# One 512-column operand for x and ctx in the key and value projection of a fused two-block transformer kernel

## The reference, cut to what matters

```python
def mixer_inputs(h, w_in_l, conv_l, ...):
    p = h @ w_in_l                       # (256, 1024) @ (1024, 2576)
    u = p[..., :512]
    qkv = silu(dwconv1d(p[..., 512:2048], conv_l))
    z = p[..., 2048:2560]
    ab = p[..., 2560:2576]               # 16 columns: the small projection
    ...
def first_block(x, c, ctx, c_ctx, w_ada, ...):
    mod_l = silu(c) @ w_ada + b_ada      # modulation vectors, 6 x 1024
    mod_c = silu(c_ctx) @ w_ada + b_ada
    hl = rmsnorm(x, g) * (1 + scale_l) + shift_l
    hc = rmsnorm(ctx, g) * (1 + scale_c) + shift_c
    ul, zl, ql, kl, vl, bl, gl = mixer_inputs(hl, ...)
    uc, zc, qc, kc, vc, bc, gc = mixer_inputs(hc, ...)   # of ctx only k, v and the gates are used
    ...
```

## Time and profile before

| what | value |
|---|---|
| time of the runs | 1788.62 us median of 3 (1787.31 to 1790.93) |
| span of the profiled execution, first to last instruction | 1786.7 us |
| the profiled execution's own time | not listed beside the span; the median stands 1.9 us above the span |
| mean granted TensorE clock | 0.988 of full speed |
| TensorE matmul busy | 1704.3 us, 95% of the span |
| VectorE busy | 1097.3 us, 61% |
| ScalarE busy | 813.0 us, 46% |

### The profile page before, as it was taken

One profiled execution on the slowest core, in us unless ns is written; L12 is line 12 of the kernel. 1 busy time (PEld: TensorE's weight loads), 2 busy tenths in 40 slices (PEclk: granted clock), 3 DMA queues, 4 the chain that ended last, 5 costly groups with the idle time before them and its releaser, 6 DMA issues.

```text
span 1786.7 us, 34649 instructions
## 1 busy us (share of the span) xinstructions
PE 1704.3 (95%) x15394; PEld 1606.0 (90%) x15394; DVE 1097.3 (61%) x1367; ACT 813.0 (46%) x1051; POOL 34.2 (2%) x68
## 2 busy tenths in 40 slices
PE   5998899999999899999999999999999999999997
PEld 4896788799988899999999899979999999979997
DVE  3476664679853565468775755555447778666463
ACT  3245414433333535447654444435454575445352
POOL 0000000000000000000000000000000000000000
PEclk8998999999999999999999999999999999999999
DMA  9676433654568444445555355525444445535552
GB/s 397 254 279 235 183 147 128 235 191 167 201 224 328 173 164 162 139 149 178 177 189 182 117 191 196 189 98 186 142 142 165 165 166 189 189 110 185 200 189 71
DMA packets 45210, 329.32 MB, mean 184 GB/s; under 512 B 5008, under 2 KB 5008, under 8 KB 5392
## 3 DMA queue, kind: packets, MB, share of 16 engines
q1 hardware_dynamic: 35712, 258.63, 41.8%
q0 software_dynamic: 9216, 67.11, 9.8%
q10 hardware_dynamic: 144, 1.51, 0.2%
HBM read 326.18 MB, written 1.05 MB: 183 GB/s over the span
## 4 chain that ended last, share of the span: by engine, by line
PE 81%; DVE 9%; ACT 6%; DMA 2%; issue 1%; POOL 0%; SPq 0%; ACTq 0%; DVEq 0%; POOLq 0%
PE ps L342 20%; PE ps L344 20%; PE ps L343 20%; PE ps L395 4%; DVE w_lo L1607 3%; PE ps L467 3%; ACT w_hi L1071 3%; PE ps L446 3%; DMA ada_raw<-ada 2%; PE ps L630 1%; PE ps L641 1%; DVE rstd L1654 1%; DVE x L1692 1%; PE ps L973 1%; DVE rsq L2334 1%
## 5 line engine op out<-in xcount | busy, mean ns | idle before, releaser
L1607 DVE TENSOR_TENSOR w_lo<-raw,w_hi 128x2048 fp32r<-128x2048 f32 x207 | 474.5, 2292 | 489.4 <-ACT w_hi L1071 489.0
L342 PE MATMUL ps<-act_hi,w_hi 128*128 128x256 f32 x2672 | 756.6, 283 | 15.0 <-DVE act_lo L1676 4.6
L343 PE MATMUL ps<-act_lo,w_hi 128*128 128x256 f32 x2672 | 744.9, 279 | 0.0
L344 PE MATMUL ps<-act_hi,w_lo 128*128 128x256 f32 x2672 | 744.8, 279 | 0.0
L1071 ACT ACTIVATE w_hi<-raw 128x2048 fp32r<-128x2048 f32 (+1 forms) x229 | 421.7, 1842 | 551.5 <-PE ps L344 549.0
L342 PEld LDWEIGHTS ps<-act_hi,w_hi 128*128 128x128 f32 x2672 | 504.1, 189 | 25.3 <-issue 16.3
L343 PEld LDWEIGHTS ps<-act_lo,w_hi 128*128 128x128 f32 x2672 | 505.4, 189 | 1.1 <-issue 0.2
L344 PEld LDWEIGHTS ps<-act_hi,w_lo 128*128 128x128 f32 x2672 | 503.6, 188 | 0.0
L342 PE MATMUL ps<-mlp_hi,w_hi 128*128 128x256 f32 x512 | 143.0, 279 | 0.2
L343 PE MATMUL ps<-mlp_lo,w_hi 128*128 128x256 f32 x512 | 141.5, 276 | 0.0
L344 PE MATMUL ps<-mlp_hi,w_lo 128*128 128x256 f32 x512 | 141.5, 276 | 0.0
(11 more groups left out here) (407 smaller groups left out, 2053.3 us busy)
## 6 DMA issues: line engine op xcount, KB each, us to landing
raw<-stream SPq DMA_DIRECT2D x233, 1024.0 KB, 4.9
ada_raw<-ada POOLq DMA_DIRECT2D x64, 1024.0 KB, 7.0
ada_f<-ada SPq DMA_DIRECT2D x4, 1024.0 KB, 14.9
ada_a<-ada SPq DMA_DIRECT2D x3, 1024.0 KB, 20.6
consts_stage<-consts_a SPq DMA_DIRECT2D x1, 1728.0 KB, 32.7
consts_stage<-consts_b ACTq DMA_DIRECT2D x1, 1472.0 KB, 10.6
x<-xT SPq DMA_DIRECT2D x1, 1024.0 KB, 7.9
xc<-ctxT SPq DMA_DIRECT2D x1, 1024.0 KB, 9.9
```

Source lines behind the costliest of these rows:

```text
L342: mm(out, ah, bh, start=first, stop=False, skip_group_check=shared)
L343: mm(out, ah, bl, start=False, stop=False, skip_group_check=shared)
L344: return mm(out, al, bh, start=False, stop=last, skip_group_check=shared)
L1607: tt(w_lo[:, s2, :], raw[:, s4, :], w_hi[:, s2, :].bitcast(f32), ALU.subtract).then_inc(S("lo_ready"), 1)
```

## The change

The four activation buffers become one tensor of the same bytes, `act_parts`, indexed by part (high, low) and by token set (ctx, x). For KV0 to KV3 a new function issues one pass of 512 columns (256 of ctx, 256 of x, two runs 8 KB apart in a partition) for each weight tile where two passes of 256 stood. An output tile `b` now fills a whole bank, and ScalarE's copy reads the banks with the two token sets inside a bank. The work that stood between the two halves of KV0 goes behind KV0, and that inside KV1 goes ahead of KV1. The wait for the last ctx tile goes ahead of KV0.

```diff
-        act_hi = [at(f"act_hi{i}", [P, KT, T], F[i], f32r) for i in range(2)]
-        act_lo = [at(f"act_lo{i}", [P, KT, T], F[2 + i], f32r) for i in range(2)]
+        act_parts = at("act_parts", [P, 2, 2, KT, T], F[0], f32r)
+        act_hi, act_lo = ([act_parts[:, part, i, :, :] for i in range(2)] for part in range(2))
...
+            def both_chunk(wp, bank):
+
+                for b in range(2):
+                    for k in range(KT):
+                        o = (b * KT + k) * P
+                        last = mm3(ps[:, bank + b, :], w_hi[:, wp, o:o + P], w_lo[:, wp, o:o + P],
+                                   act_parts[:, 0, :, k, :], act_parts[:, 1, :, k, :], k == 0, k == KT - 1)
+                return last
...
             for c in range(4):
                 n = N_KV + c
                 begin(n, n)
-                bank = KV_BANK[c]
-                feat_chunk(n % 2, bank + 1, 1)
+                if c == 0:
+                    pe.wait_ge(S("mod_lo"), 16)
+                if c == 1:
+                    pe.wait_ge(S("ab_rows"), 1)
+                    small_tr(ab_rows, 4, 16).then_inc(S("ab_mm"), 1)
+                both_chunk(n % 2, KV_BANK[c]).then_inc(S("chunk_done"), 1)
                 if c == 0:
                     pe.wait_ge(S("sw_wide"), 1)
-                    pe.wait_ge(S("mod_lo"), 16)
                     small_mm(xc, 0)
                     small_mm(norm_h1, T).then_inc(S("ab_rows_mm"), 1)
                     ada_mm(1)
-                if c == 1:
-                    pe.wait_ge(S("ab_rows"), 1)
-                    small_tr(ab_rows, 4, 16).then_inc(S("ab_mm"), 1)
-                feat_chunk(n % 2, bank, 0).then_inc(S("chunk_done"), 1)
                 ada_mm(2 + c)
...
                 act_(pre_kv[:, 2 * c:2 * c + 2, :, 1:T + 1],
-                     ps[:, bank:bank + 2, :].rearrange("p s (b t) -> p b s t", b=2), ACT.Copy).then_inc(S("evicted"), 1)
+                     ps[:, bank:bank + 2, :].rearrange("p b (s t) -> p b s t", s=2), ACT.Copy).then_inc(S("evicted"), 1)
```

## The result

The changed kernel takes 1793.58 us (median of 7 runs, 1790.29 to 1798.61), the kernel before 1785.31 (7 runs, 1780.05 to 1790.93): ratio 1.0056, 95% interval 1.0039 to 1.0073. That is slower by 10 us (0.0056 x 1785.3), with 7 to 13 in the interval. The prediction was +5.6. Its absolute time, 1794.2, lies close to the measured one by luck: its base, 1788.62 from three runs, was 3.3 above what seven runs give. Its sign and the wait that it named were right, its size was about half, and one of its steps was wrong.

A forecast was written before the change was run, and what follows sets the result against it. The prediction took TensorE, with 81% of the chain, to bound the kernel. It summed +6.5 (KV1 begins late), +1.5 (clock) and -2.4 (KV1 to KV3) to +5.6: 1788.6 + 5.6 = 1794.2 us, range 1790.0 to 1798.5.

The forecast's parts named there:

- the wait that it named: Ahead of KV1, `ada_mm(2)` right behind `ada_mm(1)` waits for its refill; TensorE idle from 73.9 to 79.0.
- Step 1: Ahead of KV0: the first wide pass needs all ctx tiles, so KV0 starts at about 59.75, +2.4 us.
- Step 2: KV0 to KV3: 192 wide passes at 0.215 us each save 1.0 us in KV0 and 2.4 in KV1 to KV3.
- width gains nothing: Rival for KV0 to KV3: a wide pass takes 0.236 us, 3.4 us of gain are lost, 1797.6; chance 0.10.
- Step 3: Behind KV0: `small_mm` 1.75 us, `ada_mm(1)` 1.87 without its 1.17 wait; refills issued at 73.4 and 74.2.
- Step 4: `ada_mm(2)` waits for refills landing at 79.0 and 81.5; KV1's work begins at 82.5, +6.5 us including earlier delays and savings.
- Step 5: Half clock behind TensorE's idle time at `ada_mm(2)` costs 1.5 us, bounds 0 and 3; nothing for the gap ahead of KV0.
- Edits at no cost: ScalarE's copy, `small_tr` heading KV1, the later refill waits and reading two runs 8 KB apart add nothing further.
- both gaps bring the clock down: Rival: low clock costs 2 us more at KV0 and up to 1.5 more at KV1, 1796 to 1798; chance 0.13.
- last test: The `ada_mm` behind KV3 comes some 5.6 us later than 114.53, and that delay is found at the kernel's end.

The follow-up runs named there:

- the fillers: The changed kernel plus dummy products on TensorE, three ahead of the wait for ctx and six between `ada_mm(1)` and `ada_mm(2)`; ratio 1.0037 to the kernel before.

## Why the prediction was right or wrong

- **Step 1, right in kind.** The gap is there and VectorE releases it. It is 3.4 instead of 2.4 us because in this execution TensorE's chain came to it 2.0 us earlier and VectorE's only 1.0 earlier (58.72 against 59.70). The gap was 2.24 to 3.99 in the executions here that have it.
- **Step 2, wrong.** The price of a wide pass was taken from f32 passes of 256 columns, 0.215. It is 0.233, the rival's "width gains nothing". So the gain of 3.4 us isn't there: KV2 and KV3 with their `ada_mm` take 26.5 us (98.61 to 125.12), against 26.3 before (88.19 to 114.53). A price borrowed from another number format stood in for a missing row; the upper bound, two narrow passes, was the better value. The figure of the Trainium skill for a dense stream ("TensorE: Matmul & The Clock Gate", Back-to-back issue gap), about 131 ns for 512 columns, is not seen in any of these kernels either.
- **Step 3, right.** `small_mm` 1.75, `ada_mm(1)` 1.91 without its wait, the refills issued at 74.62 and 75.49.
- **Step 4, right.** First half 5.1 us after its issue (5.6 was taken, 5.1 was the lower bound); the second half 2.47 us behind the first, 2.5 predicted. Moving `ada_mm(1)` alone showed the wait without the wide passes.
- **Step 5, mis-sized.** 1.5 was taken. The parts of S give 1.1 in KV0, 0.9 in the second half of `ada_mm(2)`, 0.9 in `small_tr` and 1.4 in KV1, 4.3 in all; the fillers lowered S by 3.7. The cover for the gap ahead of KV0, a gap of 2.42 us that cost no clock, failed: 3.44 us did.
- **Edits at no cost, right.** `small_tr` follows `ada_mm(2)` with no idle time between, and one run or two of operand has one price.

In S the prediction is 7.0 short (5.6 against 12.56): 1.1 from step 1, 3.4 and some 0.2 from step 2, 2.8 from step 5, less 0.5 from step 4. The forecast's wait and two of its rivals, "width gains nothing" and "both gaps bring the clock down", came true together. They were given as cases that exclude each other, though nothing in them does; the rivals' own prices, 3.4 and up to 3.5, added to the 5.6 come to 12.5.

Its last test was that the delay behind KV3 be found at the end. That delay is 10.6 us (125.12 against 114.53). All runs together show it, 7 to 13; the two profiled executions alone, with 4.8 at the end, would not have.

## What to carry to other kernels

A stream with two buffers needs other work between two of its consumers, as long as issue, transfer and contention of one refill; moving one consumer behind the next turns hidden loads into a wait, whatever the move was for. For an operation with no row, the row of the same format is a better price than one of another format. Price an idle gap on TensorE with the slow work behind it, and try a filler of products in the gaps: here that alone was worth 0.27% (0.07 to 0.46).

## What was not expected of the hardware

- The narrow passes have two paces, 0.113 and 0.118 us, a whole chunk at a time, at a granted clock of 1.00; which chunk gets which differs between executions of one kernel. The cause stays open.
- Gaps of 2.24 to 3.99 us ahead of KV0 were followed by half clock (KV0 waiting for ctx had 0.67 from 60 to 65 behind 2.97 us), and one of 2.42 us elsewhere was not the earlier trace rows. What tells them apart is open.
- In after the clock stood at 0.50 from 236 to 246 us with TensorE busy all the time, behind small products of 64 columns and an idle time of 1.63 us at 232.94. Before had an idle time of 1.31 us at the same place and kept 1.00, and the two groups of products there took 3.9 us each instead of 6.3. Why is open.
